# Tokens gathered as rows in f32, y scattered in two f32r halves, glu columns finished first: one change to the expert stage of a hybrid attention and mixture-of-experts block

## The chip, the cores and the metric

The kernel runs on one core of a Trainium2 chip. The metric is the time of one execution on the device in microseconds (us). The kernel before takes 1219.95 us, the median of 3 runs (1217.81 to 1220.06).

The engines: PE (TensorE) multiplies, PEld is its weight load, DVE is VectorE, ACT is ScalarE, POOL is GpSimd. SP issues nearly all of the big transfers (DMA).

## The reference

One layer: RMSNorm, a projection into forgetting attention, short convolution and cross-attention, their gated merge into x1, then a mixture of experts. The change touches the mixture and what chooses its tokens.

```python
def clamped_swiglu(h):
    glu, lin = h[..., :D_FF], h[..., D_FF:]
    glu = jnp.minimum(glu, SWIGLU_LIMIT)
    lin = jnp.clip(lin, -SWIGLU_LIMIT, SWIGLU_LIMIT)
    return glu * jax.nn.sigmoid(SWIGLU_ALPHA * glu) * (lin + 1.0)

def moe(x2, w_router, b_router, w_up, b_up, w_down, b_down):
    logits = (x2 @ w_router + b_router).astype(jnp.float32)
    top_vals, top_idx = lax.top_k(logits, TOP_K)
    top_w = jax.nn.softmax(top_vals, axis=-1)
    combine = ...                       # top_w at the chosen experts, 0 elsewhere
    out = jnp.zeros_like(x2)
    for e in range(N_EXPERTS):
        a = clamped_swiglu(x2 @ w_up[e] + b_up[e])
        out = out + combine[:, e:e + 1] * (a @ w_down[e] + b_down[e])
    return out

h2 = rms_norm(x1, norm2_g, NORM_EPS).reshape(B * S, D)     # return x1 + moe(h2, ...)
```

Sizes: 256 tokens, D = 1024, 32 experts with d_ff = 1024, 4 experts to a token, all in f32. The weights of one expert are 12 MiB.

## The kernel before

**Stages.** The first 270 us or so are the dense part: pieces of weights are loaded, split into f32r halves (`w_hi`, `w_lo`) and multiplied as hi x hi + lo x hi + hi x lo. Then come the routing and the experts.

**The ring.** Expert weights stream through a ring of 11 slots of 2 MiB in SBUF. A chunk fills a slot. An expert is 6 chunks: 4 of `w_up` (two of the eight row blocks k = 0..7 each, 2048 columns: 1024 glu, 1024 lin) and 2 of `w_down` (four row blocks each). SP issues the 192 loads in order. Load g waits until PE has finished with load g - 11, and a load is otherwise bound by nothing. Slots 0 to 9 are taken from buffers of the dense part as these fall free. The eleventh holds `h2T` and `x1s`, and its first load waits for the routing to be done with them (`parts_pool`, `parts_dve`).

**The routing** (lines 1110 to 1190 on DVE). DVE waits for the logits, takes the top 8 (`max`), their indices (`max_index`), casts these to f32 (L1129), builds one-hot rows for four experts and sums them to `chosen`. PE turns `chosen` into positions with a triangular product. `pos_tab` then holds each token's place in each expert's list of 64 slots. `more` is the number of further lists that experts with over 64 tokens need. The trace has 32 lists, so there were none.

**One item** is one expert's list of 64 slots. PE's order of work in `item` (L1590):

1. Up product, k = 0..7: for each k the glu and the lin columns, two halves of 512 each. The 64 slots of a half take 64 output partitions, so two matmuls stand side by side (`bank_glu`, `bank_lin`).
2. Behind k = 6, `gather` (L1537) for the next item: tokens of x1, scaled and split in three bf16 parts (`m_parts`), times the one-hot `pick`. It is 48 matmuls of 64 columns, and gives the features on partitions at once (`bank_cy`), which DVE moves to `xgT` with the norm's gain (L1164).
3. `scatter` (L1587) of the item before into three of its four output banks: the token weights `pick_wT` (f32) times `y_sb` (f32).
4. Transposes of the activated rows `sig` to `aT` (L1635), which wait for `a_ready`. Then the fourth bank's scatter, two transposes of `pick_w` (L1644), the bias rows (L1650), and the down product (L1661) of 16 matmuls.

**Activation between 3 and 4.** When all of the up product is done (`up_done`), DVE clamps glu (L1224), clamps lin (L1225), multiplies (lin + 1) with glu (L1228), and multiplies with ACT's Sigmoid (L1232), which signals `a_ready`. ACT's round is: Sigmoid, copy of `aT`, copy of `pick_wT`, copy of `y_sb`. DVE and ACT run items in a hardware loop, PE's 32 items are written out. Each engine runs its instructions in the order written, and waits on semaphores.

## Time and profile before

| | |
|---|---|
| median of 3 runs | 1219.95 us |
| the profiled execution's own time | 1219.87 us |
| its span (first to last instruction) | 1218.1 us |
| PE busy | 1169.7 us (96%) |
| DVE, ACT, POOL busy | 339.1, 266.9, 84.7 us |
| PE's granted clock, mean over the span | 0.978 |
| DMA | 450.16 MB; 427 to 428 GB/s from 330 us to 1150 us |
| chain that ended last | PE 85%, DVE 10%, ACT 2% |

A busy PE is not PE at its peak: matmuls overlap, and their ends are modelled. Read an item by the starts of its groups, which add up without gaps. A matmul in f32 shows as two records. "Granted clock" is 1.0 at 2.4 GHz and 0.5 at 1.2 GHz. An item starts with its first L1604 matmul: 288.76 us for the first, 1211 us is the end of the last down product.

### The profile page before, as it was taken

The numbers are of one execution on the slowest core, as the hardware profiler recorded it, in microseconds if no ns is written. First come the engines' busy times: TensorE is split into PE (matmuls) and PEld (weight loads), VectorE is DVE, ScalarE is ACT, GpSimd is POOL, SyncE is SP. The second block draws the span as 40 slices with busy tenths as digits, with TensorE's granted clock in tenths as the row PEclk, the third lists the DMA queues.
The fourth block names the chain that finished last, engine by engine and source line by source line (L and its number), as shares of the span: only waits on it lengthen the run. The fifth ranks groups of instructions, "written<-read, shape, count | busy, mean of one in ns | idle before, by whom it ended". The sixth has DMA issues, their size and how long they took to land.

```text
span 1218.1 us, 15891 instructions
## 1 busy us (share of the span) xinstructions
PE 1169.7 (96%) x6786; PEld 562.5 (46%) x6788; DVE 339.1 (28%) x625; ACT 266.9 (22%) x407; POOL 84.7 (7%) x101
## 2 busy tenths in 40 slices
PE   8999999997999999999999999999999999999998
PEld 7789988884333333333333333333333333333332
DVE  5767865655111111111111111111121111111112
ACT  6765454442111111111111111111111111111110
POOL 6333340001000000000000000000000000000000
PEclk9999999998999999999999999999999999999999
DMA  8454469858999999999999999999999999999991
GB/s 313 151 169 149 151 246 361 304 217 330 382 425 429 428 428 428 427 428 426 429 427 427 428 428 429 426 427 428 427 428 428 427 427 428 428 426 427 428 405 66
DMA packets 51476, 450.16 MB, mean 370 GB/s; under 512 B 4610, under 2 KB 4738, under 8 KB 26836
## 3 DMA queue, kind: packets, MB, share of 16 engines
q1 hardware_dynamic: 49936, 447.76, 89.1%
q10 hardware_dynamic: 1476, 1.42, 0.4%
q8 instruction: 55, 0.90, 0.3%
q14 instruction: 9, 0.07, 0.0%
HBM read 448.12 MB, written 1.05 MB: 369 GB/s over the span
## 4 chain that ended last, share of the span: by engine, by line
PE 85%; DVE 10%; ACT 2%; issue 1%; POOL 1%; DMA 0%; DVEq 0%; SPq 0%; POOLq 0%; ACTq 0%
PE aux L1604 37%; PE aux L1661 20%; PE acc L1448 11%; PE aux L1537 4%; PE acc L1441 3%; PE acc L1587 3%; PE aux L1635 2%; DVE lin L1228 2%; DVE sig L1232 2%; DVE glu L1224 2%; DVE lin L1225 2%; PE aux L1615 1%; DVE w_lo L880 1%; PE aux L1650 1%; PE aux L1644 1%
## 5 line engine op out<-in xcount | busy, mean ns | idle before, releaser
L1604 PE MATMUL aux<-ring,xgT 128*64 128x512 f32 x2048 | 458.2, 594 | 0.8 <-DVE xgT L1164 0.8
L1604 PEld LDWEIGHTS aux<-ring,xgT 128*64 128x64 f32 x2048 | 140.5, 137 | 266.4 <-issue 258.0
L1661 PE MATMUL aux<-ring,aT 128*64 128x512 f32 x1024 | 245.3, 635 | 0.0
L1224 DVE TENSOR_SCALAR glu<-aux 128x512 f32<-128x512 f32 x32 | 22.1, 692 | 483.3 <-PE aux L1604 483.3
L1661 PEld LDWEIGHTS aux<-ring,aT 128*64 128x64 f32 x1024 | 77.0, 147 | 148.7 <-issue 147.1
L845 ACT ACTIVATE sig<-glu 128x512 f32<-128x512 f32 x32 | 20.1, 630 | 474.9 <-DVE glu L1224 474.9
L880 DVE TENSOR_TENSOR w_lo<-raw,w_hi 128x1024 fp32r<-128x1024 f32 x80 | 104.3, 1324 | 50.0 <-ACT w_hi L662 50.0
L662 ACT ACTIVATE w_hi<-raw 128x1024 fp32r<-128x1024 f32 x80 | 84.1, 1059 | 88.6 <-PE acc L1448 73.0
L1587 PE MATMUL acc<-y_sb,pick_wT 64*128 64x512 f32 x256 | 98.2, 628 | 0.8 <-ACT y_sb L853 0.8
L1448 PE MATMUL acc<-w_hi,hT_hi 128*128 128x512 f32 x188 | 75.7, 403 | 1.4 <-DVE hT_lo L892 1.3
L1448 PE MATMUL acc<-w_hi,hT_lo 128*128 128x512 f32 x188 | 73.3, 390 | 0.0
L1448 PE MATMUL acc<-w_lo,hT_hi 128*128 128x512 f32 x188 | 73.2, 390 | 0.0
L1160 DVE TENSOR_SCALAR bias_sel<-ones_bf,exp_sel 96x64 bf16<-96x64 bf16 x33 | 7.8, 237 | 233.0 <-PE aux L1661 233.0
L853 ACT ACTIVATE y_sb<-aux 128x512 f32<-128x512 f32 x32 | 19.1, 598 | 238.1 <-PE aux L1661 238.1
L1537 PEld LDWEIGHTS aux<-pick,m_parts 128*128 128x128 bf16 x1584 | 49.2, 99 | 26.9 <-issue 26.0
L1537 PE MATMUL aux<-pick,m_parts 128*128 128x64 bf16 x1584 | 53.1, 195 | 0.4 <-DVE pick L1150 0.4
L1635 PE MATMUL aux<-ident,sig 128*128 128x128 f32 x128 | 24.0, 310 | 30.2 <-DVE sig L1232 30.2
L1587 PEld LDWEIGHTS acc<-y_sb,pick_wT 64*128 64x128 f32 x256 | 30.8, 185 | 45.8 <-issue 42.1
L1635 PEld LDWEIGHTS aux<-ident,sig 128*128 128x128 f32 x128 | 17.9, 209 | 56.0 <-DVE sig L1232 56.0
L845 ACT ACT_TABLE_LOAD x32 | 41.1, 1283 | 0.6
L1448 PEld LDWEIGHTS acc<-w_hi,hT_hi 128*128 128x128 f32 x188 | 35.3, 188 | 9.4 <-issue 1.6
L1448 PEld LDWEIGHTS acc<-w_hi,hT_lo 128*128 128x128 f32 x188 | 35.3, 188 | 7.6
(292 smaller groups left out, 920.1 us busy)
## 6 DMA issues: line engine op xcount, KB each, us to landing
ring<-w_up_dram SPq DMA_DIRECT2D x128, 2048.0 KB, 22.9
ring<-w_down_dram SPq DMA_DIRECT2D x64, 2048.0 KB, 21.9
raw<-w_in_dram SPq DMA_DIRECT2D x25, 1024.0 KB, 5.2
raw<-w_branch_dram SPq DMA_DIRECT2D x6, 1024.0 KB, 5.2
raw<-w_kv_dram SPq DMA_DIRECT2D x4, 1024.0 KB, 5.2
raw<-w_out_dram SPq DMA_DIRECT2D x4, 1024.0 KB, 5.3
x<-x_dram SPq DMA_DIRECT2D x2, 512.0 KB, 4.3
raw<-w_in_dram SPq DMA_DIRECT2D x2, 512.0 KB, 6.4
```

The costliest lines, as they stand in the source:

```text
L662: nc.scalar.activation(w_hi[:, s % 4], raw[:, p % 4, 2 * h:2 * h + 2], ACT.Copy).then_inc(hi_done, 1)
L845: nc.scalar.activation(sig[:], glu[:], ACT.Sigmoid, scale=ALPHA).then_inc(sig_ready, 1)
L880: nc.vector.tensor_tensor(w_lo[:, s % 4], raw[:, p % 4, 2 * h:2 * h + 2], plain_f32(w_hi[:, s % 4]), ALU.subtract).then_inc(lo_done, 1)
L1224: nc.vector.tensor_scalar(glu[:], bank_glu[:], LIMIT, None, ALU.min).then_inc(glu_ready, 1)
L1225: nc.vector.tensor_scalar(lin[:], bank_lin[:], LIMIT, -LIMIT, ALU.min, ALU.max).then_inc(up_read, 1)
L1441: ins = nc.tensor.matmul(dst, w_[:, cs], a_[:, k], start=opening and m == 0 and c % 2 == 0, stop=closing and m == 2, skip_group_check=True)
L1448: ins = nc.tensor.matmul(banks[t][:], a_[:, k, ts], w_, start=opening and m == 0 and kind != "gate", stop=closing and m == 2)
L1537: ins = nc.tensor.matmul(bank_cy[:, k * SLOTS:(k + 1) * SLOTS], up_rows(m_parts[:, m, t], k), pick[:, t], start=(t == 0 and m == 0 and k = ...
L1587: nc.tensor.matmul(acc[b][:], pick_wT[s, t], y_sb[s, :], start=False, stop=True, skip_group_check=True).then_inc(scattered, 1)
L1604: ins = nc.tensor.matmul(bank[64 * half:64 * half + 64, :], xgT[:, k], w_rows[:, c0 + half * W:c0 + (half + 1) * W], start=(k == 0), stop= ...
L1635: ins = nc.tensor.transpose(bank_t[:, j * P:(j + 1) * P], sig[:].rearrange("s (p j) -> s j p", j=DOWN_ROWS)[:, j], ident[:])
L1661: ins = nc.tensor.matmul(bank_cy[64 * half:64 * half + 64, :], aT[:, j, 64 * ff_half:64 * ff_half + 64], w_rows[:, half * W:(half + 1) * W ...
```

## The change

- **Gather by tokens.** `pick` is now f32 and carries the token's `rstd`. It is the stationary operand, x1 itself in f32 is the moving one: 4 matmuls of 512 columns that give the 64 rows of the list (`bank_cy`). ACT copies them to SBUF (`xg_tok`, the same memory as `sig`), PE turns them with 4 transposes, and DVE moves them to `xgT`. The parts `m_parts`, `x1s` and what built them are gone. The gather for the next item stands behind k = 3, the turn behind k = 5.
- **Glu first.** For the last chunk (k = 6, 7) all glu columns come first and signal `glu_done`, then the lin columns, which signal `up_done`. DVE clamps glu, multiplies it with the Sigmoid, and only then clamps lin, in PSUM, and multiplies.
- **Scatter in f32r halves.** ACT writes y scaled with the slot's weight as `y_hi`, DVE the remainder as `y_lo`. The stationary operand is the 0/1 matrix `pickT` in f32r. It is 8 f32r matmuls, all ahead of the transposes of `sig`. They belong to the item before, which was so before too.
- **The transposes of `pick_w`** move into the middle of the down product; DVE makes `pickT` and `slot_w` from them.
- **Chosen by match-replace.** The four chosen logits are overwritten with a marker, and a comparison gives `chosen`. Softmax is taken over all 32 logits and masked.
- **A twelfth slot**, in the memory that `hT_lo`, `merged` and `m_parts` had. `hT_lo` and `merged` move into slot 10, which is first loaded behind the last dense product. Slot 11 waits for `logits_ready`.

ACT's loop, one round, before: the row that loads a function table stands at the head and has no wait in front of it.

```order
L855 UNCONDITIONAL_BRANCH
L845 ACT_TABLE_LOAD
L845 ACTIVATE sig<-glu 128x512 [waits glu_ready]
L847 ACTIVATE aT<-aux 128x512 [waits aT_done]
L849 REGISTER_ALU [waits pick_wT_done]
L850 ACTIVATE pick_wT<-aux 128x256 [waits scattered]
L853 ACTIVATE y_sb<-aux 128x512 [waits y_done]
L855 REGISTER_ALU
L855 COMPARE_AND_BRANCH
```

The same loop after the change:

```order
L827 ISA
L812 ACT_TABLE_LOAD
L812 ACTIVATE sig<-aux 128x512 [waits gathered]
L820 ACT_TABLE_LOAD [waits glu_ready]
L820 ACTIVATE sig<-glu 128x512 [waits xg_turned]
L822 ACTIVATE aT<-aux 128x512 [waits aT_done]
L825 ACTIVATE y_hi<-aux,slot_w 128x512 [waits y_done,pickT_ready]
L827 REGISTER_ALU
L827 COMPARE_AND_BRANCH
```

There are now two table rows in a round, one for the copy at the head and one for the Sigmoid. The second is behind the wait for `glu_ready`, and the Sigmoid itself waits for `xg_turned`.

PE, the second item of before from the gather to the bias rows of the down product:

```order
L1537 MATMUL aux<-pick,m_parts 128x64 [waits y_ready,pick_ready]
L1537 MATMUL aux<-pick,m_parts 128x64 x47
L1604 MATMUL aux<-ring,xgT 64x512 x4
L1587 MATMUL acc<-y_sb,pick_wT 128x512 [waits pick_wT_ready,y_ready]
L1587 MATMUL acc<-y_sb,pick_wT 128x512 x2
L1635 MATMUL aux<-ident,sig 128x128 [waits pick_wT_ready,a_ready]
L1635 MATMUL aux<-ident,sig 128x128 x3
L1587 MATMUL acc<-y_sb,pick_wT 128x512 [waits pick_wT_ready,y_ready]
L1644 MATMUL aux<-ident,pick_w 128x128 [waits aT_ready,pick_w_ready]
L1644 MATMUL aux<-ident,pick_w 128x128
L1650 MATMUL aux<-bias_down,bias_sel 64x512 [waits xg_ready]
L1650 MATMUL aux<-bias_down,bias_sel 64x512
```

PE, the second item after the change, from the end of the up product into the down product (`acc` are the four output banks):

```order
L1551 MATMUL acc<-y_hi,pickT 128x512 [waits y_lo_ready,y_hi_ready,pickT_ready]
L1551 MATMUL acc<-y_hi,pickT 128x512
L1551 MATMUL acc<-y_lo,pickT 128x512 x2
L1551 MATMUL acc<-y_hi,pickT 128x512 x2
L1551 MATMUL acc<-y_lo,pickT 128x512 x2
L1613 MATMUL aux<-ident,sig 128x128 [waits a_ready]
L1613 MATMUL aux<-ident,sig 128x128 x3
L1619 MATMUL aux<-bias_down,bias_sel 64x512 [waits xg_ready]
L1619 MATMUL aux<-bias_down,bias_sel 64x512
L1631 MATMUL aux<-ring,aT 64x512 [waits slot_loaded10,aT_ready]
L1631 MATMUL aux<-ring,aT 64x512 x7
L1642 MATMUL aux<-ident,pick_w 128x128 [waits pick_w_ready]
```

The scatter is whole and ahead of `a_ready`. Nothing but the two bias rows stands between the transposes of `sig` and the down product, which now waits for `aT_ready` itself. The first row of the `pick_w` transposes is behind eight matmuls of the down product.

PE, the same item's up product after the change, from k = 2:

```order
L1561 MATMUL aux<-ring,xgT 64x512 [waits slot_loaded7]
L1561 MATMUL aux<-ring,xgT 64x512 x7
L1494 MATMUL aux<-x_50,pick 64x512 [waits pick_ready,y_lo_ready,y_hi_ready]
L1494 MATMUL aux<-x_50,pick 64x512 x3
L1561 MATMUL aux<-ring,xgT 64x512 [waits slot_loaded8]
L1561 MATMUL aux<-ring,xgT 64x512 x7
L1506 MATMUL aux<-ident,sig 128x128 [waits xg_tok_ready]
L1506 MATMUL aux<-ident,sig 128x128 x3
L1561 MATMUL aux<-ring,xgT 64x512 [waits slot_loaded9]
L1561 MATMUL aux<-ring,xgT 64x512 x7
```

The gather (L1494) and the turn (L1506) stand between groups of matmuls of the up product. The last group of eight is glu, then lin, of k = 6 and 7.

The diff, cut to its core (names of semaphores, memory and routing tables are left out where the list above says it):

```diff
             sp.wait_ge(half_used, 2 * NP)
-            load_next(8)
-            load_next(9)
+            for g in (8, 9, 10):
+                load_next(g)
             sp.wait_ge(logits_ready, 1)
-            sp.wait_ge(parts_pool, 2)
-            sp.wait_ge(parts_dve, 2)
-            load_next(10)
+            load_next(11)
...
+            def copy_gathered(n):
+                act.wait_ge(gathered, n)
+                nc.scalar.activation(xg_tok[:], bank_cy[:], ACT.Copy).then_inc(xg_tok_ready, 1)
+
+            copy_gathered(1)
 
             def item(n):
+                copy_gathered(n + 1)
+                act.wait_ge(xg_turned, n + 1)
                 act.wait_ge(glu_ready, n)
                 nc.scalar.activation(sig[:], glu[:], ACT.Sigmoid, scale=ALPHA).then_inc(sig_ready, 1)
                 act.wait_ge(aT_done, n)
                 nc.scalar.activation(aT[:].rearrange("p k s -> p (k s)"), bank_t[:], ACT.Copy).then_inc(aT_ready, 1)
-                act.wait_ge(pick_wT_done, n)
-                act.wait_ge(scattered, 4 * n)
-                nc.scalar.activation(pick_wT[:].rearrange("p t s -> p (t s)"), bank_t[:, 0:NT * P],
-                                     ACT.Copy).then_inc(pick_wT_ready, 1)
+                act.wait_ge(pickT_ready, n)
                 act.wait_ge(y_done, n)
-                nc.scalar.activation(y_sb[:], bank_cy[:], ACT.Copy).then_inc(y_ready, 1)
+                nc.scalar.activation(y_hi[:], bank_cy[:], ACT.Copy, scale=slot_w[:, 0:1]).then_inc(y_hi_ready, 1)
 
...
+            nc.vector.tensor_scalar(ntop[:], top_v[:, :, 0], -1.0, None, ALU.mult).then_inc(top_ready, 1)
+
+            chained(nc.vector.memset(top_v[:, :, TOPK:8], HUGE))
             for t in range(NT):
-                ins = nc.vector.max_index(top_i[:, t], top_v[:, t], logits[:, t])
+                ins = nc.vector.match_replace(out=others[:, t], in_to_replace=top_v[:, t], in_values=logits[:, t],
+                                              imm_value=-HUGE)
             chained(ins)
-            chained(nc.vector.tensor_copy(top_f[:], top_i[:]))
+            nc.vector.tensor_scalar(chosen3[:, :, 0], others[:], -HUGE, None, ALU.is_equal).then_inc(chosen_ready, 1)
+            dve.wait_ge(chosen_ready, 1)
+            chosen = chosen3[:, :, 0]
...
             def item(n):
 
+                dve.wait_ge(glu_done, n)
+                nc.vector.tensor_scalar(glu[:], bank_glu[:], LIMIT, None, ALU.min).then_inc(glu_ready, 1)
+                dve.wait_ge(glu_ready, n)
+                dve.wait_ge(sig_ready, n)
+                nc.vector.tensor_tensor(sig[:], glu[:], sig[:], ALU.mult).then_inc(gated_ready, 1)
                 dve.wait_ge(up_done, n)
-                nc.vector.tensor_scalar(glu[:], bank_glu[:], LIMIT, None, ALU.min).then_inc(glu_ready, 1)
-                nc.vector.tensor_scalar(lin[:], bank_lin[:], LIMIT, -LIMIT, ALU.min, ALU.max).then_inc(up_read, 1)
-                dve.wait_ge(glu_ready, n)
-                dve.wait_ge(up_read, n + 1)
-                nc.vector.scalar_tensor_tensor(lin[:], lin[:], 1.0, glu[:], ALU.add, ALU.mult
-                                               ).then_inc(glin_ready, 1)
-                dve.wait_ge(glin_ready, n)
-                dve.wait_ge(sig_ready, n)
-                nc.vector.tensor_tensor(sig[:], lin[:], sig[:], ALU.mult).then_inc(a_ready, 1)
-
-                dve.wait_ge(gathered, n + 1)
-                move_gathered()
+                nc.vector.tensor_scalar(bank_lin[:], bank_lin[:], LIMIT, -LIMIT, ALU.min, ALU.max
+                                        ).then_inc(lin_ready, 1)
+                dve.wait_ge(gated_ready, n)
+                dve.wait_ge(lin_ready, n)
+                nc.vector.scalar_tensor_tensor(sig[:], bank_lin[:], 1.0, sig[:], ALU.add, ALU.mult
+                                               ).then_inc(a_ready, 1)
+
+                move_gathered(n + 1)
+                build_pick_w(bass.ds(n - 1, 1))
                 build_pick(bass.ds(n + 1, 1))
+
                 dve.wait_ge(pick_wT_done, n)
-                build_pick_w(bass.ds(n, 1))
+                nc.vector.tensor_scalar(pickT[:].rearrange("p t s -> p (t s)"), bank_t[:, 0:NT * P], 0.0, None,
+                                        ALU.is_gt)
+                nc.vector.tensor_reduce(slot_w[:], bank_t[:, 0:NT * P], AX, ALU.add).then_inc(pickT_ready, 1)
                 dve.wait_ge(y_done, n)
                 build_bias_sel(bass.ds(n, 1))
+                dve.wait_ge(pickT_ready, n)
+                dve.wait_ge(y_hi_ready, n)
+                nc.vector.scalar_tensor_tensor(y_lo[:], bank_cy[:], slot_w[:, 0:1], plain_f32(y_hi[:]),
+                                               ALU.mult, ALU.subtract).then_inc(y_lo_ready, 1)
 
             with dve.Fori(1, NEXP + 1) as n:
...
-            def gather(first_item=False):
-
+
+            def gather(n):
+
+                pe.wait_ge(pick_ready, n)
                 for t in range(NT):
-                    for m in range(3):
-                        if first_item and t == 1 and m == 2:
-                            pe.wait_ge(parts_dve, 2)
-                        for k in range(KD):
-                            ins = nc.tensor.matmul(bank_cy[:, k * SLOTS:(k + 1) * SLOTS],
-                                                   up_rows(m_parts[:, m, t], k), pick[:, t],
-                                                   start=(t == 0 and m == 0 and k == 0),
-                                                   stop=(t == NT - 1 and m == 2), skip_group_check=True)
+            def turn_gathered(n):
+
+                pe.wait_ge(xg_tok_ready, n)
+                for q in range(KD // 2):
+                    c, j = q // UP_ROWS, q % UP_ROWS
+                    n = UP_ROWS * P
+                    rows = xg_tok[:, c * n:(c + 1) * n].rearrange("s (p j) -> s j p", j=UP_ROWS)[:, j]
+                    ins = nc.tensor.transpose(bank_cy[:, q * P:(q + 1) * P], rows, ident[:])
+                ins.then_inc(xg_turned, 1)
...
-            def scatter(items, banks):
-
-                pe.wait_ge(y_ready, items)
-                pe.wait_ge(pick_wT_ready, items - 1)
-                for b in banks:
-                    t, half = b // 2, b % 2
-                    s = slice(64 * half, 64 * half + 64)
-                    nc.tensor.matmul(acc[b][:], pick_wT[s, t], y_sb[s, :],
...
+            def scatter(n, opening=False):
+
+                pe.wait_ge(pickT_ready, n)
+                pe.wait_ge(y_hi_ready, n)
+                pe.wait_ge(y_lo_ready, n)
+                for t in range(NT):
+                    for part in (y_hi, y_lo):
+                        for half in range(2):
+                            s = slice(64 * half, 64 * half + 64)
+                            ins = nc.tensor.matmul(acc[2 * t + half][:], pickT[s, t], part[s, :],
+                                                   start=opening and part is y_hi, stop=True, skip_group_check=True)
+                            if part is y_lo:
+                                ins.then_inc(scattered, 1)
...
+                    if k == 3:
+                        if not first_item:
+                            pe.wait_ge(y_hi_ready, n - 1)
+                            pe.wait_ge(y_lo_ready, n - 1)
+                        gather(n + 1)
+                    if k == 5:
+                        turn_gathered(n + 1)
+
+                c = UP_CHUNKS - 1
+                pe.wait_ge(slot_loaded[slot_of[c]], loads[c])
+                for bank, c0, done in ((bank_glu, 0, glu_done), (bank_lin, FF, up_done)):
+                    for k in range(KD - UP_ROWS, KD):
+                        ins = up_product(k, bank, c0)
+                    ins.then_inc(done, 1)
 
                 if not first_item:
-                    scatter(n, range(3))
...
+                pe.wait_ge(aT_ready, n)
```

## Rows read from the trace of the kernel before

**Rows 1.** Stretches, all engines: items 3, 4, 2 to 32, two early gaps.

```profile
core 0: us, PE busy (x) PEld busy (x) DVE busy (x) ACT busy (x) POOL busy (x), PEclk, DMA share, GB/s
347.70:377.45 29.75, 28.82 (x168) 10.44 (x165) 4.44 (x10) 3.49 (x5) 0.00 (x0) 0.94 1.01 428
377.45:405.50 28.05, 27.12 (x168) 10.01 (x165) 4.44 (x10) 3.49 (x5) 0.00 (x0) 1.00 1.01 428
319.71:1211.00 891.29, 862.38 (x5086) 317.26 (x5082) 137.58 (x310) 108.27 (x155) 0.00 (x0) 0.98 0.98 417
282.00:290.00 8.00, 4.88 (x58) 3.57 (x61) 6.01 (x21) 2.97 (x8) 0.50 (x1) 0.57 0.54 187
...
314.00:320.00 6.00, 6.00 (x30) 1.96 (x28) 0.00 (x0) 0.07 (x1) 0.00 (x0) 1.00 0.59 183
```

**Rows 2.** PE in order of time, item 4: start, us, line, what, count, idle.

```profile
390.00 1.57 PE L1537 MATMUL aux<-pick,m_parts 128*128 128x64 bf16 x48
391.50 1.94 PE L1604 MATMUL aux<-ring,xgT 128*64 128x512 f32 x8
393.37 1.98 PE L1587 MATMUL acc<-y_sb,pick_wT 64*128 64x512 f32 x6
396.29 0.75 PE L1635 MATMUL aux<-ident,sig 128*128 128x128 f32 x4 [0.93 <-DVE sig L1232]
...
398.63 7.03 PE L1661 MATMUL aux<-ring,aT 128*64 128x512 f32 x32
405.50 1.02 PE L1604 MATMUL aux<-ring,xgT 128*64 128x512 f32 x4
```

**Rows 3.** ACT in order of time, the same item.

```profile
377.66 0.60 ACT L853 ACTIVATE y_sb<-aux 128x512 f32<-128x512 f32 x1 [8.23 <-PE aux L1661]
378.28 1.28 ACT L845 ACT_TABLE_LOAD   x1
394.21 0.63 ACT L845 ACTIVATE sig<-glu 128x512 f32<-128x512 f32 x1 [14.65 <-DVE glu L1224]
397.07 0.60 ACT L847 ACTIVATE aT<-aux 128x512 f32<-128x512 f32 x1 [2.23 <-PE aux L1635]
```

**Rows 4.** DVE in order of time, the same item.

```profile
393.49 0.69 DVE L1224 TENSOR_SCALAR glu<-aux 128x512 f32<-128x512 f32 x1 [15.48 <-PE aux L1604]
394.10 0.68 DVE L1225 TENSOR_SCALAR lin<-aux 128x512 f32<-128x512 f32 x1
394.81 0.69 DVE L1228 SCALAR_TENSOR_TENSOR lin<-lin,glu 128x512 f32<-128x512 f32 x1
395.54 0.69 DVE L1232 TENSOR_TENSOR sig<-lin,sig 128x512 f32<-128x512 f32 x1
```

**Rows 5.** PE in order of time, f32r matmuls of the dense part.

```profile
263.17 0.39 PE L1448 MATMUL acc<-w_lo,hT_hi 128*128 128x512 f32 x1
263.39 0.39 PE L1448 MATMUL acc<-w_hi,hT_lo 128*128 128x512 f32 x1
```

**Rows 6.** DVE in order of time, in the routing.

```profile
280.15 0.40 DVE L1120 SCALAR_TENSOR_TENSOR logits<-acc,rstd,spread 128x32 f32<-128x32 f32 x2
...
281.36 1.17 DVE L1129 CAST top_f<-top_i 128x16 f32<-128x16 uint32 x1
```

**Rows 7.** PE in order of time, from the router to the first expert.

```profile
275.11 1.94 PE L1486 MATMUL acc<-wr,h2T 128*128 128x32 f32 x16 [0.25 <-DVE h2T L1102]
...
285.24 2.74 PE L1537 MATMUL aux<-pick,m_parts 128*128 128x64 bf16 x48 [0.44 <-DVE pick L1150]
288.76 1.12 PE L1604 MATMUL aux<-ring,xgT 128*64 128x512 f32 x2 [0.78 <-DVE xgT L1164]
```

**Rows 8.** ACT in order of time, the last copy of y.

```profile
1211.04 0.60 ACT L853 ACTIVATE y_sb<-aux 128x512 f32<-128x512 f32 x1 [6.75 <-PE aux L1661]
```

**Rows 9.** The last load into the ring: its issue, and its time to landing.

```profile
L452 SPq DMA_DIRECT2D ring<-w_down_dram x1: 327/327/327, 1157.1 to 1157.1; - x1
...
DMA to landing us min/median/max: 36.0/36.0/36.0
```

More of the change, by code:

```diff
@@ L1552, in list_first @@
+            turn_gathered(1)
             def list_first():
@@ L1590, in item @@
-            def item(n, slot_of, loads, between={}):
-                first_item = bool(between)
+            def scatter(n, opening=False):
[4 more added lines that the diff above has]
+                    for part in (y_hi, y_lo):
+                        for half in range(2):
+                            s = slice(64 * half, 64 * half + 64)
[3 more added lines that the diff above has]
+                                ins.then_inc(scattered, 1)
@@ new lines, in item, with up_product @@
+            def item(n, slot_of, loads, first_item=False, second_item=False):
+                def up_product(k, bank, c0):
+                    w_rows = ring[:, slot_of[k // UP_ROWS]].rearrange("p (j n) -> p j n", j=UP_ROWS)[:, k % UP_ROWS]
+                    for half in range(2):
+                        ins = nc.tensor.matmul(bank[64 * half:64 * half + 64, :], xgT[:, k],
+                                               w_rows[:, c0 + half * W:c0 + (half + 1) * W],
+                                               start=(k == 0), stop=(k == KD - 1), skip_group_check=True)
+                    return ins
```

264 lines of the change are left out of this document (101 added, 163 removed).

## The prediction

> **What bounds the kernel now.** I read four views in this order: the slices of the page, the stretches, the order of time of one item, and the ring's loads.
>
> The stretches first [rows 1]. Items 2 to 32 take 891.29 us of the 1218.1 us span, with PE busy for 862.38 us and the DMA engines at a share of 0.98. So both limits are near. Item 4, at a granted clock of 1.00, takes 28.05 us. Item 3 has a mean clock of 0.94 and takes 29.75 us. 31 items at 28.05 would be 869.6 us, so the clock costs 21.7 us, or some 13 drops of 1.70 us each.
>
> The item [rows 2]. PE never waits for a chunk. Its one wait with a releaser is at 396.29, where the transposes of `sig` wait 0.93 us for DVE. The last up product ends at 391.50 + 1.94 = 393.44, and the transposes start 2.85 us later. In those 2.85 us lies the chain of four DVE operations [rows 4], with ACT's Sigmoid beside it [rows 3]. The three banks of scatter cover some 2 us of it. So PE sets the pace, and inside an item it is the chain from the end of the up product to `a_ready`.
>
> The other limit is close. The last load is issued at 1157.1 and lands 36.0 us later, at 1193.1 [rows 9], while PE's last down product ends at 1211 [rows 8]. An item's 12 MiB (12.58 MB) at the 428 GB/s of [rows 1] take 29.4 us, more than the item on PE, which the queue of issued loads makes up for so far. So a faster PE would gain only until it meets the transfers.
>
> **The change part by part.** All sums are against the profiled execution: 1219.87 us, 1.8 us more than its span, and within 0.1 us of the median 1219.95. A matmul of the product kind (f32, 512 columns, two side by side) costs (405.50 - 398.63) / 16 = 0.43 us [rows 2].
>
> *Before, one item at full clock, by starts* [rows 2]: gather 391.50 - 390.00 = 1.50; from the last product's slot to the transposes 396.29 - 393.37 = 2.92; from there to the down product 398.63 - 396.29 = 2.34; all else 28.05 - 6.76 = 21.29.
>
> *Gather and turn.* Four matmuls of the product kind, 4 x 0.43 = 1.72 us. Four transposes, 0.75 us as the ones at 396.29, and 0.05 for the edges: 0.80. ACT's copy between them takes 0.60 us [rows 3] and has two k (3.4 us) of products as cover, so it is free. The wait of the gather for `y_lo` is free too: y is ready some 1.5 us into the item, the gather comes after 7 us. Bounds for the turn: 0.75 to 1.0.
>
> *From the glu columns to `a_ready`.* This is the step that decides. The listing of ACT's loop shows a table row behind the wait for `glu_ready`. In the trace of before the table load takes 1.28 us, but it starts at 378.28, right behind the copy of y and 15 us ahead of the Sigmoid [rows 3]. Now it stands in the chain. From `glu_done`: clamp of glu 0.69, table load 1.28, Sigmoid 0.63, product with glu 0.69, clamp of lin 0.68, last product 0.69, and six handoffs of 0.03 to 0.05 as in [rows 3, 4], less the 0.07 that back-to-back DVE rows overlap (393.49 to 394.10): 4.84 us. DVE waits in order, so the clamp of lin, whose input has long been there, also stands behind the load. Glu is done four matmuls, 1.72 us, before the end of the up product. From that end to the transposes it is 4.84 - 1.72 = 3.12 us, against 2.85 before. So that step is 2.92 + 0.27 = 3.19. The head start of 1.72 and the shorter tail are eaten by the load. The clamp in PSUM is not in the trace; 0.4 (a small one) to 0.9 bounds it, I take the 0.68 of the PSUM to SBUF one.
>
> *Scatter.* Eight f32r matmuls at a spacing of 263.39 - 263.17 = 0.22 us [rows 5] are 1.8 us, or 0.9 if the two halves, which use different rows of the array, run side by side. Both fit in the 3.12 us. Cost nothing; and the fourth bank (about 1.06 of the 2.34) is gone from behind the transposes. But it was that matmul that covered ACT's copy of `aT`.
>
> *Transposes to down product.* ACT starts 397.07 - 396.29 = 0.78 after the transposes, copies 0.60, handoff 0.05: 1.43 us, with the bias rows inside. Before 2.34.
>
> *Transposes of `pick_w` inside the down product.* Half of the four at 396.29, 0.37, and two edges: 0.50 (0.37 to 0.7).
>
> *New item at full clock:* 21.29 + 1.72 + 0.80 + 3.19 + 1.43 + 0.50 = 28.93 us, so **+0.88 us** an item and +28.2 us for 32. With the bounds of the terms it is +0.4 to +1.3.
>
> *Clock.* Before, an item has one gap of 0.93 us without a matmul, and 13 of 31 items show a drop. Now the gaps are 3.12 - 1.8 = 1.3 us ahead of the transposes and about 0.5 us (0.78 + 0.60 + 0.05 less 0.67 of transposes and 0.25 of bias rows) behind them: 1.8 us within 4.6 us. In proportion that is 1.9 x 13/31 = 0.8 of the items, 25 drops, 12 more at 1.67 us: **+20.0 us**. Bounds: none more (0) and one in every item (19 more, +31.7).
>
> *Start.* The router's products end at 275.11 + 1.94 = 277.05 [rows 7], but DVE takes the logits at 280.15 [rows 6], since it is busy with the parts: -3.1. The cast goes, -1.2 [rows 6]. One-hot, sum and index over 256 columns give way to operations on 64, about -0.9. The gather falls from 2.74 (at the half clock) to 1.72, -1.0 [rows 7]. Copy, turn and handoffs are new, +1.5. Sum **-4.7 us** (-2 to -6). The first up product then starts near 284 instead of 288.76.
>
> *End.* Behind the last copy of y comes one DVE operation and its handoff, +0.75, and 1.8 us of scatter instead of 2.0: **+0.6 us**.
>
> *The twelfth slot* lets loads start earlier: shares of 0.54 in 282 to 290 and 0.59 in 314 to 320 [rows 1] are 3.7 + 2.5 = 6.2 us of idle transfers. It is worth nothing while PE sets the pace, and 6.2 us if the transfers do. DVE's and POOL's other operations (`pickT`, `slot_w`, `pick_w`) have 3 us and more of the down product as cover.
>
> *Sum:* 1219.87 - 4.7 + 28.2 + 20.0 + 0.6 = **1264 us**.
>
> *A rule beside it.* In the trace the copy of y ends at 378.26 and the load starts at 378.28 and is over after 1.28 [rows 3], so there is no drain to be seen. The Trainium skill (ScalarE: Activation LUTs, What ACT_TABLE_LOAD costs) gives the same 1283 ns and adds about 1380 ns of drain for each switch. By that the chain would be 1.38 us longer and the sum would be 1308 us. The trace does not bear it out.
>
> **The rivals.**
>
> *The load isn't in the chain* (it costs nothing when run, or goes ahead of the wait). Then the chain is 3.56 us, the scatter just fills the 1.84 us behind the up product, and an item is 27.65 us at full clock. PE then meets the transfers: the last load lands at 1193.1 - 6.2 = 1186.9, then half a down product (3.4 us) and what follows 1211 now (7.1 + 0.6 us) give 1198.0 of span, **1200 us**. For it speaks that a reload for a copy seems needless, against it the listing, in which a load at the head of the loop and one behind `glu_ready` are real rows, and that each such row of before shows as 1.28 us. The Trainium skill (ScalarE: Activation LUTs, Table sets: the hidden batching unit) says that cheap functions such as the copy are in every set; by that one set would do, and this rival's time would hold. No row here shows a copy that runs in the Sigmoid's set and loads nothing.
>
> *The clock takes no more than before.* The item is longer but the drops stay 13: 1264 - 20 = **1244 us**. For it: two short gaps may count for less than one long one, and the later start of the down product moves the gaps about. Against it: the time without a matmul doubles.
>
> *The clock falls in every item, or twice in some.* If the halves of the scatter run side by side, the first gap is 2.2 us. One in each item gives **1276 us**, a few twice up to 1285.
>
> *Terms that cancel.* The item grows only by 0.2 (turn and transposes overlap, a fast clamp) and the drops stay: 1219.9 - 4.7 + 6.4 + 0.6 = 1222 us.
>
> **How the numbers follow.** The forecast of 1264 (1252 to 1272) has 0.50. Clock as before: 0.20. Clock in every item or more, drain included: 0.17. Terms that cancel: 0.04. The load out of the chain: 0.09. A difference below 0.2%, 2.4 us, can't be told from none here. Faster holds the load's rival: 0.09. No difference: 0.03, out of the terms that cancel. The rest, 0.88, is slower. The range of 1228 to 1280 leaves out the rival at 1200, the no-change case and the highest times, together some 0.16. Its low end is the sum with the low bound of the item (+0.4, 12.8 us) and no added drop.
>
> **What would show each step.** The profile after should have a table load between the clamp of glu and the Sigmoid in each item, PE's idle time ahead of the transposes of `sig` with releaser DVE at 1.1 to 1.4 us (or 2 us, if the scatter's halves overlap), and some 0.5 us ahead of the down product with releaser ACT. Item starts at full clock should be 28.9 us apart and the mean clock over the items 0.95 to 0.96. At some 30.3 us an item, over the transfers' 29.4, the DMA share should fall below 1, and a load should land in 8 to 15 us late in the run too: the ring then waits for PE. The first up product should start near 284. If instead PE waits for chunks late in the run and loads take 40 us and more to land, the transfers bound it and the forecast is wrong. It is wrong too if the table load runs ahead of `glu_ready`, or if the clock stays at 1.0.

## The result and the profile after

| | median us | range | runs |
|---|---|---|---|
| before | 1218.88 | 1217.57 to 1220.06 | 4 |
| after | 1282.73 | 1281.22 to 1283.16 | 4 |

The ratio is 1.0522, with a 95% interval of 1.0504 to 1.0540: 63.8 us slower. The forecast was 1264 us, the range 1228 to 1280. The direction was right. The time lies 2.7 us above the range.

The page of the kernel after (engines' busy time with count, then the slices; in the groups, busy us and mean ns of one, then idle time and its releaser; for the loads, KB and median us to landing). Its own time is 1281.22 us:

```profile
span 1279.4 us, 13646 instructions
...
PE 1182.9 (92%) x5596; PEld 549.9 (43%) x5596; DVE 380.8 (30%) x711; ACT 313.6 (25%) x432; POOL 80.2 (6%) x98
...
DMA  8545489679999999999999999999999999999900
...
L820 ACT ACT_TABLE_LOAD x32 | 41.1, 1283 | 198.5 <-DVE glu L1180 198.5
...
ring<-w_up_dram SPq DMA_DIRECT2D x128, 2048.0 KB, 12.3
```

PE is busy for 92% of the span instead of 96%. The table load stands in each of the 32 items behind `glu`, and costs 1283 ns. A load of the ring lands 12.3 us after its issue: the ring waits for PE now, and PE for no transfer.

The stretches of the kernel after (item 2, and items 2 to 32; columns as in [rows 1]), to be held against the 28.05, 29.75 and 891.29 us of [rows 1]:

```profile
318.88:349.60 30.72, 28.22 (x130) 9.95 (x128) 5.98 (x13) 5.08 (x6) 0.00 (x0) 0.94 0.98 409
318.88:1271.40 952.52, 874.91 (x3970) 307.14 (x3966) 185.55 (x403) 157.45 (x186) 0.00 (x0) 0.94 0.93 387
```

All 31 items are 30.72 to 30.74 us long (952.52 / 31 = 30.73), and all have a mean clock of 0.94. Before, only some had.

PE in order of time over an item of the kernel after, from its turn of the gathered rows to the next item (start, us, line, what, count, idle), the counterpart of [rows 2]:

```profile
449.11 1.89 PE L1494 MATMUL aux<-x,pick 128*64 128x512 f32 x8
450.83 3.60 PE L1561 MATMUL aux<-ring,xgT 128*64 128x512 f32 x16
454.36 0.74 PE L1506 MATMUL aux<-ident,sig 128*128 128x128 f32 x4
455.04 3.65 PE L1561 MATMUL aux<-ring,xgT 128*64 128x512 f32 x16
458.62 0.50 PE L1551 MATMUL acc<-y_hi,pickT 64*128 64x512 f32 x2
458.95 0.40 PE L1551 MATMUL acc<-y_lo,pickT 64*128 64x512 f32 x2
459.19 0.40 PE L1551 MATMUL acc<-y_hi,pickT 64*128 64x512 f32 x2
459.42 0.40 PE L1551 MATMUL acc<-y_lo,pickT 64*128 64x512 f32 x2
461.98 0.75 PE L1613 MATMUL aux<-ident,sig 128*128 128x128 f32 x4 [2.16 <-DVE sig L1189]
462.65 0.41 PE L1619 MATMUL aux<-bias_down,bias_sel 96*64 96x512 bf16 x2
463.41 5.35 PE L1631 MATMUL aux<-ring,aT 128*64 128x512 f32 x16 [0.35 <-ACT aT L822]
468.69 0.44 PE L1642 MATMUL aux<-ident,pick_w 128*128 128x128 f32 x2
469.06 3.65 PE L1631 MATMUL aux<-ring,aT 128*64 128x512 f32 x16
```

Two things are to be seen. The eight matmuls of the scatter start in pairs, 0.24 us apart, so they are over after 1.2 us, and PE then waits 2.16 us. And the first eight down matmuls (16 records) take 5.35 us, the second eight 3.65: the slow stretch of the clock lies in the first half of the down product. Its granted clock, ahead of it, in it and behind it (columns as in [rows 1]):

```profile
462.00:463.70 1.70, 1.35 (x8) 0.84 (x10) 1.47 (x5) 0.60 (x1) 0.00 (x0) 0.98 0.97 414
464.00:467.00 3.00, 3.00 (x10) 0.96 (x8) 0.00 (x0) 0.00 (x0) 0.00 (x0) 0.50 1.02 431
467.10:470.00 2.90, 2.90 (x16) 0.86 (x14) 0.76 (x2) 0.00 (x0) 0.00 (x0) 1.00 1.00 356
```

PE works at 1.2 GHz instead of 2.4 right after the two waits, and that costs 5.35 - 3.65 = 1.70 us. Such a stretch at the lower clock is called a drop here. Without it an item takes 30.72 - 1.70 = 29.02 us.

ACT and DVE over the same stretch, the counterpart of [rows 3, 4]:

```profile
457.79 1.28 ACT L820 ACT_TABLE_LOAD   x1 [6.15 <-DVE glu L1180]
459.08 0.63 ACT L820 ACTIVATE sig<-glu 128x512 f32<-128x512 f32 x1
462.76 0.60 ACT L822 ACTIVATE aT<-aux 128x512 f32<-128x512 f32 x1 [3.04 <-PE aux L1613]
```

```profile
457.02 0.69 DVE L1180 TENSOR_SCALAR glu<-aux 128x512 f32<-128x512 f32 x1 [13.38 <-PE aux L1561]
459.82 0.69 DVE L1183 TENSOR_TENSOR sig<-glu,sig 128x512 f32<-128x512 f32 x1 [2.11 <-ACT sig L820]
460.43 0.69 DVE L1185 TENSOR_SCALAR aux<-aux 128x512 f32<-128x512 f32 x1
461.23 0.69 DVE L1189 SCALAR_TENSOR_TENSOR sig<-aux,sig 128x512 f32<-128x512 f32 x1
```

This is the chain as forecast: clamp of glu, load, Sigmoid, three DVE operations, 461.98 - 457.02 = 4.96 us to the transposes.

Start and end (PE, the first gather, the first up product, the last scatter), the counterparts of [rows 7, 8]:

```profile
279.71 3.42 PE L1494 MATMUL aux<-x,pick 128*64 128x512 f32 x8 [0.72 <-DVE pick L1111]
...
285.36 1.94 PE L1561 MATMUL aux<-ring,xgT 128*64 128x512 f32 x8 [0.79 <-DVE xgT L1129]
...
1273.43 0.50 PE L1551 MATMUL acc<-y_hi,pickT 64*128 64x512 f32 x2 [1.80 <-DVE y_lo L1204]
```

The spans differ by 1279.4 - 1218.1 = 61.3 us. Start: 285.36 - 288.76 = -3.4. Item 1: (318.88 - 285.36) - (319.71 - 288.76) = +2.6. Items 2 to 32: 952.5 - 891.3 = +61.2. End: (1279.4 - 1271.4) - (1218.1 - 1211.0) = +0.9. Within the +61.2, 31 items are 29.02 - 28.05 = 0.97 us longer at full clock, 30.1 us. The drops are 31 x 1.70 = 52.7 us against 21.7 before, +31.0. Item 1 has a drop in both kernels.

### The profile page after: what moved, and what is told of

Read it like the earlier page. It is cut to its first block, busy times and chain, and to the rows that moved or that the text cites. A ratio compares the mean times of both kernels' runs of the same rounds, so it can differ in the third digit from the quotient of the medians.

```text
span 1279.4 us, 13646 instructions
## 1 busy us (share of the span) xinstructions
PE 1182.9 (92%) x5596; PEld 549.9 (43%) x5596; DVE 380.8 (30%) x711; ACT 313.6 (25%) x432; POOL 80.2 (6%) x98
## 4 chain that ended last, share of the span: by engine, by line
PE 80%; DVE 10%; ACT 8%; issue 2%; POOL 1%; DMA 0%; DVEq 0%; ACTq 0%; SPq 0%; POOLq 0%
PE aux L1561 31%; PE aux L1631 22%; PE acc L1413 11%; PE aux L1494 5%; ACT L820 3%; PE acc L1406 3%; PE aux L1613 2%; DVE sig L1189 2%; DVE glu L1180 2%; DVE sig L1183 2%; PE aux L1506 2%; ACT sig L820 2%; DVE aux L1185 2%; ACT aT L822 2%; PE aux L1581 1%
## 5 line engine op out<-in xcount | busy, mean ns | idle before, releaser
L1561 PE MATMUL aux<-ring,xgT 128*64 128x512 f32 x2048 | 463.5, 594 | 0.8 <-DVE xgT L1129 0.8
L1631 PE MATMUL aux<-ring,aT 128*64 128x512 f32 x1024 | 288.0, 714 | 11.2 <-ACT aT L822 11.2
L1561 PEld LDWEIGHTS aux<-ring,xgT 128*64 128x64 f32 x2048 | 143.7, 137 | 264.3 <-issue 253.8
L1631 PEld LDWEIGHTS aux<-ring,aT 128*64 128x64 f32 x1024 | 80.0, 160 | 177.7 <-issue 157.0
L825 ACT ACTIVATE y_hi<-aux,slot_w 128x512 fp32r<-128x512 f32 x32 | 22.0, 687 | 302.7 <-PE aux L1631 302.7
L820 ACT ACT_TABLE_LOAD x32 | 41.1, 1283 | 198.5 <-DVE glu L1180 198.5
L812 ACT ACTIVATE sig<-aux 128x512 f32<-128x512 f32 x33 | 19.7, 597 | 231.5 <-PE aux L1494 231.5
L1197 DVE TENSOR_SCALAR pickT<-aux 128x256 fp32r<-128x256 f32 x32 | 13.6, 424 | 182.0 <-PE aux L1642 182.0
L1494 PE MATMUL aux<-x,pick 128*64 128x512 f32 x264 | 63.8, 605 | 0.7 <-DVE pick L1111 0.7
L822 ACT ACTIVATE aT<-aux 128x512 f32<-128x512 f32 x32 | 19.1, 597 | 97.4 <-PE aux L1613 97.4
L1183 DVE TENSOR_TENSOR sig<-glu,sig 128x512 f32<-128x512 f32 x32 | 22.2, 693 | 67.4 <-ACT sig L820 67.4
L812 ACT ACT_TABLE_LOAD x32 | 41.1, 1283 | 0.6
## 6 DMA issues: line engine op xcount, KB each, us to landing
ring<-w_up_dram SPq DMA_DIRECT2D x128, 2048.0 KB, 12.3
```

What stands on the lines that cost most here:

```text
L812: nc.scalar.activation(xg_tok[:], bank_cy[:], ACT.Copy).then_inc(xg_tok_ready, 1)
L820: nc.scalar.activation(sig[:], glu[:], ACT.Sigmoid, scale=ALPHA).then_inc(sig_ready, 1)
L822: nc.scalar.activation(aT[:].rearrange("p k s -> p (k s)"), bank_t[:], ACT.Copy).then_inc(aT_ready, 1)
L1183: nc.vector.tensor_tensor(sig[:], glu[:], sig[:], ALU.mult).then_inc(gated_ready, 1)
L1494: ins = nc.tensor.matmul(bank_cy[64 * half:64 * half + 64, :], pick[:, t], x1[:, t, half * W:(half + 1) * W], start=(t == 0), stop=(t == N ...
L1561: ins = nc.tensor.matmul(bank[64 * half:64 * half + 64, :], xgT[:, k], w_rows[:, c0 + half * W:c0 + (half + 1) * W], start=(k == 0), stop= ...
```

## The experiments

All stand against runs of the kernel before on the same chip (median 1217.86 to 1218.05). The theory: the longer item comes from the table load in the chain, and the rest from the clock, which falls in proportion to PE's idle time. The rivals: the load costs nothing there, or the clock falls in each item whatever the size of the gap.

**The load ahead of the wait.** ACT's two waits are exchanged. In the kernel after, the load stood behind the one that is written second, `glu_ready`; with the order turned round it stands behind `xg_turned`, which comes earlier.

```diff
-                act.wait_ge(xg_turned, n + 1)
                 act.wait_ge(glu_ready, n)
+                act.wait_ge(xg_turned, n + 1)
```

> The changed kernel with ACT's two waits ahead of the Sigmoid swapped, so that the table load stands behind xg_turned and no longer behind glu_ready. Theory (the load of 1.28 us is in the chain, and the longer gap makes the clock fall in every item): the chain from glu_done to the transposes falls from 4.96 to 3.7 us, the gap on PE from 2.3 to about 1.0 us, an item at full clock is 27.7 us, the drops fall to 13 of 31 or fewer, and the transfers bound the stage: 1200 us (1193 to 1212), DMA share 1.0, last loads landing after 40 us and more. Rival (the load isn't what makes the item long; gather, turn and the uncovered copy of aT are): only a few us less, 1265 to 1280 us.

Measured: 1200.78 us (1198.17 to 1201.96), ratio 0.9849 (0.9828 to 0.9869). Two waits exchanged turn +5.2% into -1.5%. ACT in this kernel, then PE:

```profile
470.72 1.28 ACT L820 ACT_TABLE_LOAD   x1 [3.54 <-PE aux L1506]
473.28 0.63 ACT L820 ACTIVATE sig<-glu 128x512 f32<-128x512 f32 x1 [1.28 <-DVE glu L1180]
```

```profile
476.17 0.75 PE L1613 MATMUL aux<-ident,sig 128*128 128x128 f32 x4 [0.81 <-DVE sig L1189]
...
477.61 3.65 PE L1631 MATMUL aux<-ring,aT 128*64 128x512 f32 x16 [0.35 <-ACT aT L822]
```

The load is over before `glu_ready` comes. The gap falls from 2.16 to 0.81 us, and the down product runs at full clock. The stretches (one item, and the items up to 1060 us):

```profile
457.35:485.05 27.70, 26.54 (x131) 9.51 (x129) 5.99 (x13) 5.08 (x6) 0.00 (x0) 1.00 1.01 428
315.00:1060.00 745.00, 710.31 (x3418) 254.35 (x3418) 157.39 (x342) 135.85 (x160) 0.00 (x0) 1.00 1.01 427
```

An item is 27.70 us, 1.32 less than the 29.02, which is the load of 1.28. None of items 2 to 32 has a drop. 32 x 1.32 + 31 x 1.70 = 95 us would come back, and 82 did, since the transfers now bound the end: from item 25 on an item takes 29.4 us, what its 12 MiB take at 428 GB/s. PE's waits for loads over the whole span (us, times, longest):

```profile
PE aux L1561 <- DMA ring<-w_up_dram: 9.4, 17, 1.1
```

**The gap filled.** The kernel after, with matmuls of no use between the scatter and the wait for `a_ready`:

```diff
+                    for _ in range(9):
+                        nc.tensor.matmul(bank_t[:], ones_bf[0:96], bias_up[:, 0:W], start=True, stop=True)
```

> The changed kernel with nine bf16 matmuls of 512 columns (ones times the bias rows, into the bank that the transposes of sig then overwrite) between the scatter and the wait for a_ready, items 2 to 32. They add no result. The chain stays as it is, the gap of 2.3 us is filled with 9 x 0.22 = 1.95 us of matmuls. Theory (the gap makes the clock fall, 1.71 us an item): items 29.0 us apart without drops, 1281 - 31 x 1.71 = 1228 us. Rival (the drop has another cause, say the wait for aT or the period of the item): 30.7 us apart as before, 1282 us; if the matmuls delay the transposes, more.

Measured: 1229.78 us (1228.94 to 1231.54), ratio 1.0097 (1.0079 to 1.0115).

```profile
453.51 2.12 PE L1610 MATMUL aux<-bias_up,ones_bf 96*128 96x512 bf16 x9
455.73 0.75 PE L1615 MATMUL aux<-ident,sig 128*128 128x128 f32 x4
```

The work of an item, its chain and its length at full clock are as in the kernel after. Only the time without a matmul is gone (0.10 us of it is left ahead of the transposes), and 1282.7 - 1229.8 = 52.9 us with it, against 31 x 1.70 = 52.7. Items 2 to 32 have no drop and are 29.04 us long. So the clock costs 53 us here. What is left over the kernel before (1229.78 - 1217.94 = 11.8 us) is the longer item, the start and the end, less the 21.7 us that the kernel before loses by its own drops.

**The scatter in another order**, all of one row half first (DVE's last adds then wait for the whole scatter, which is left out here):

```diff
-                for t in range(NT):
-                    for part in (y_hi, y_lo):
-                        for half in range(2):
+                for half in range(2):
+                    for t in range(NT):
+                        for part in (y_hi, y_lo):
```

> The changed kernel with the eight scatter matmuls in another order: the four of one half, then the four of the other, so that two that use the same rows of the array follow each other. (The last adds wait for all of the scatter.) Chain unchanged. Theory of the forecast (matmuls of different rows ran side by side, 0.24 us a pair, which made the gap 2.3 instead of 1.3 us, and the number of drops goes with the length of the gap): scatter 1.8 us, gap 1.3 to 1.4 us, 20 to 26 drops instead of 31, items 29.0 us at full clock, 1263 to 1275 us. Rival (any gap over a certain length costs a drop in each item): 1282 us. Rival (below that length none or few): 1235 to 1250 us.

Measured: 1282.81 us (1281.54 to 1284.01), ratio 1.0526 (1.0507 to 1.0544). It did not do what it was meant to:

```profile
461.62 0.41 PE L1551 MATMUL acc<-y_lo,pickT 64*128 64x512 f32 x2
464.18 0.75 PE L1613 MATMUL aux<-ident,sig 128*128 128x128 f32 x4 [2.15 <-DVE sig L1189]
```

The scatter still took 1.2 us and the gap stayed at 2.15, so the run tests nothing about the length of the gap. It does say that PE puts the matmuls of the two row halves side by side in this order too. The Trainium skill (TensorEngine Tiling (Array Packing), Key Properties) says that tiles of the array operate independently of each other, and both traces agree, with 0.24 us from pair to pair. The trace of the kernel before already showed it. Its first two banks of scatter, one of each row half, take 1.13 us together, and the third bank alone adds 0.85 to make the 1.98 of [rows 2]:

```profile
393.37 1.13 PE L1587 MATMUL acc<-y_sb,pick_wT 64*128 64x512 f32 x4
```

**The load put into the chain of the kernel before:**

```diff
+                act.wait_ge(up_done, n)
                 act.wait_ge(glu_ready, n)
```

> The kernel before with a second wait (up_done) ahead of the Sigmoid, which puts its table load behind glu_ready; nothing else. Theory (the load alone makes a chain long): the product with the Sigmoid starts 2.75 us after the end of the up product instead of 2.1, so the transposes start 0.66 us later, the gap grows from 0.93 to 1.6 us, items 28.7 us at full clock (+21 us), and the clock falls in 22 to 31 of 31 items instead of 13 (+15 to +31 us): 1255 to 1271 us. Rival (DVE hides the load, or it costs nothing here): 1219 us. Rival (chain longer but no more drops): 1240 us.

Measured: 1265.53 us (1264.30 to 1268.65), ratio 1.0396 (1.0374 to 1.0417). Three stretches of one item each, without a drop, with one of twice the length and with one:

```profile
400.32:429.12 28.80, 27.12 (x165) 10.11 (x165) 4.44 (x11) 3.49 (x5) 0.00 (x0) 1.00 1.00 420
368.25:400.32 32.07, 30.39 (x164) 10.71 (x164) 4.43 (x11) 3.49 (x5) 0.00 (x0) 0.89 0.97 404
409.53:439.92 30.39, 28.71 (x168) 10.48 (x166) 4.44 (x10) 3.49 (x5) 0.00 (x0) 0.94 1.00 423
```

```profile
400.32 0.75 PE L1636 MATMUL aux<-ident,sig 128*128 128x128 f32 x4 [1.68 <-DVE sig L1233]
```

The gap goes from 0.93 us to 1.68, the item from 28.05 to 28.80: 32 x 0.75 = 24 us. The clock takes about as much again: of items 2 to 32, 10 have no drop, 16 have one and 5 have one of twice the length, as in the second row (3.3 us). That is 21 items with a drop, against 13 before. The gap is 1.68 us in all of them, with a drop and without. The load at this place is thus enough for 3.9%, with no other part of the change.

**Part of the gap filled**, with four matmuls, then six (the same edit, with 4 and 6 for the 9):

> The changed kernel with four instead of nine of the filling bf16 matmuls between scatter and a_ready (0.9 us; they add no result), which leaves the gap of 1.3 us that the prediction had reckoned with. Theory of the forecast (a drop count in proportion to the gap: the step failed only because the scatter took 1.0 and not 1.8 us): 20 to 28 drops, 1258 to 1276 us. Rival (the rule of proportion itself was wrong, upwards): a drop in each item still, 1282 us. Rival (wrong downwards; the kernel with the early load had a gap of 0.8 us and no drops): 1230 to 1250 us.

> As the kernels with nine and four filling matmuls, with six: the gap ahead of the transposes is 0.75 us, the one behind them 0.35 us as before, the chain and the item (29.0 us at full clock) are the same. So far: gaps of 1.18 and 0.35 us with a drop in all 31 items, gaps of 0.1 and 0.35 with none, and the early load with 0.81 and 0.35 with none. Theory (there is a length of idle time below which no item has a drop, and above which, at this item length, each has): none, 1230 us. Rival (in proportion after all, with a steeper rule): some 10 to 20 drops, 1247 to 1264 us.

Measured with four: 1282.84 us (1282.26 to 1283.42), ratio 1.0532 (1.0513 to 1.0551). With six, in two runs: 1230.81 us (1230.54 to 1231.09), ratio 1.0106 (1.0076 to 1.0135). The transposes of `sig`, with four:

```profile
463.63 0.75 PE L1615 MATMUL aux<-ident,sig 128*128 128x128 f32 x4 [1.18 <-DVE sig L1189]
```

and with six:

```profile
456.98 0.75 PE L1615 MATMUL aux<-ident,sig 128*128 128x128 f32 x4 [0.75 <-DVE sig L1189]
```

Halving the gap gives back nothing: a drop in each of items 2 to 32, as with 2.16 us. Another 0.43 us off, and all of these drops go. In this kernel the clock's cost is a step in the gap, not a slope. It is no rule for the gap alone: the kernel before with the load in its chain has a gap of 1.68 us, well above this step, and 10 of its 31 items have no drop.

**The second gap closed as well:** the four, and one more behind the bias rows.

```diff
+                    for _ in range(4):
+                        nc.tensor.matmul(bank_t[:], ones_bf[0:96], bias_up[:, 0:W], start=True, stop=True)
...
+                nc.tensor.matmul(bank_glu[:], ones_bf[0:96], bias_up[:, 0:W], start=True, stop=True)
```

> Four filling matmuls ahead of the transposes (gap 1.18 us, with which each item had a drop) and one behind the bias rows, in the wait for aT (0.35 us falls to some 0.13 us), written to the bank of glu, which the next item starts anew. Theory (idle time of both gaps together counts: 1.31 us, between the 1.16 us without drops and the 1.53 us with one in each item): fewer drops, 1230 to 1262 us. Rival (the gap ahead of the transposes alone counts): 1282 us.

Measured, in two runs: 1283.07 us (1282.94 to 1283.20), ratio 1.0535 (1.0504 to 1.0565).

```profile
465.21 5.35 PE L1634 MATMUL aux<-ring,aT 128*64 128x512 f32 x16
```

The wait ahead of the down product is gone, and the drop is still there (5.35 us). With 1.18 us ahead of the transposes, closing the other gap changes nothing. That doesn't settle which of them counts: PE is still idle for 1.21 us of an item here, and was for 27.70 - 26.54 = 1.16 in the kernel with the early load, which has no drops in items 2 to 32. So whether the first gap or the sum of both counts stays open.

**The glu columns given no head start.** The kernel with the early load, and DVE's clamp of glu waits for all of the up product, as in the kernel before:

```diff
-                dve.wait_ge(glu_done, n)
+                dve.wait_ge(up_done, n)
```

> The kernel with the early table load, with DVE's clamp of glu waiting for up_done instead of glu_done; PE's order stays. It takes away what glu first gives. Theory (the chain from the end of the up product sets the gap): transposes 1.72 us later, gap 2.5 us, items 29.4 us at full clock and a drop in each, 31.1 us apart: 1200 -> 1285 to 1300 us. Rival (the chain is covered by something else): 1200 to 1215 us.

Measured: 1282.53 us (1281.81 to 1283.45), ratio 1.0528 (1.0509 to 1.0547). The head start is worth 81.7 us where the load is out of the chain, drops included. The expected 1285 to 1300 was missed, though the chain is longer than in the kernel after:

```profile
464.83 0.75 PE L1613 MATMUL aux<-ident,sig 128*128 128x128 f32 x4 [2.53 <-DVE sig L1189]
465.51 0.62 PE L1619 MATMUL aux<-bias_down,bias_sel 96*64 96x512 bf16 x2
466.27 4.98 PE L1631 MATMUL aux<-ring,aT 128*64 128x512 f32 x16
```

The slow stretch begins earlier here and lies partly in waiting time (the bias rows take 0.62 us instead of 0.41), so the down product loses 4.98 - 3.65 = 1.33 us instead of 1.70. By as much as the gap is longer (2.53 - 2.16 = 0.37 us) the drop is cheaper, and the item is 30.72 us again. It came to that by steps: item 2 takes 31.03 us, item 3 30.87, item 4 30.80, and from item 9 on all take 30.72. Items 2 and 10:

```profile
320.83:351.86 31.03, 28.15 (x130) 9.89 (x128) 5.98 (x13) 5.08 (x6) 0.00 (x0) 0.95 0.98 406
567.21:597.93 30.72, 28.07 (x130) 9.85 (x128) 5.99 (x13) 5.08 (x6) 0.00 (x0) 0.94 0.99 411
```

**The ring with 11 slots**, in the kernel with the early load (the memory of the twelfth stays unused):

```diff
-RING = 12
+RING = 11
...
-            sp.wait_ge(logits_ready, 1)
-            load_next(11)
```

> The kernel with the early table load, with the ring back at 11 slots (the memory of the twelfth stays unused). Theory (12 slots let the early transfers run without a break, 6 us, and the transfers set the end of this version): last landing 3 to 7 us later than with 12 slots, 1204 to 1208 us. Rival (PE sets the pace for most of the run and the transfers only late, so the idle transfers are made up for): 1200 to 1202 us.

Measured: 1202.97 us (1202.71 to 1205.14), ratio 0.9882 (0.9864 to 0.9901). It is 2.2 us over the kernel with twelve, whose own runs reach from 1198.2 to 1202.0. The last load lands at 1138.8 + 49.5 = 1188.3 instead of 1136.5 + 51.0 = 1187.5. Both ranges expected were missed, the rival's (1200 to 1202) by 1 us. The twelfth slot is worth some 2 us at most even where transfers bind, on two chips and hardly clear of the scatter of the runs, and not the 6.2 of the prediction.

**The kernel before with its gap filled**, four matmuls behind the three banks of scatter:

```diff
+                    for _ in range(4):
+                        nc.tensor.matmul(bank_t[:], ones_bf[0:96], bias_up[:, 0:W], start=True, stop=True)
```

> The kernel before with four filling bf16 matmuls (0.87 us, into the bank that the transposes overwrite; they add no result) behind the three banks of scatter, where PE waits 0.93 us for DVE. Theory (its 13 drops come from that gap and cost 21.7 us): items 28.05 us apart, clock near 1.0, and the transfers then set the end: last landing 1193 us, then half a down product and 7 us: 1200 to 1208 us. Rival (the drops have another cause): 1218 us, 13 drops as before.

Measured: 1208.93 us (1208.83 to 1210.64), ratio 0.9925 (0.9907 to 0.9943), 0.9 us over the upper end expected. The 13 drops are gone, worth 21.7 us, but only 9.1 arrive: here too the items grow to 29.4 us, from item 27 on, with the transfers as the bound. PE's waits for loads in this kernel:

```profile
PE aux L1604 <- DMA ring<-w_up_dram: 10.5, 10, 1.2
```

The last load is issued at 1145.6 and lands 48.4 us later, at 1194.0, 6.5 us after that of the kernel with the early load. That accounts for most of the 8.2 us between the two. Which part of the change lets its transfers finish earlier (the slots that no longer wait for the routing's buffers, or the earlier start) was argued, not measured.

## Why the prediction was right in its direction and short by 19 us

- **The item at full clock: right.** Forecast 28.93 us, measured 29.02. Of its terms, gather 450.83 - 449.11 = 1.72 (1.72); the turn 455.04 - 454.36 = 0.68 (0.80); from the end of the up product's slot to the transposes 461.98 - 458.62 = 3.36 (3.19); from there to the down product 1.43 (1.43); the transposes of `pick_w` 469.06 - 468.69 = 0.37 (0.50). The clamp in PSUM takes 0.69 (0.68 taken). Single terms are off by up to 0.17 us in both directions, and the rest of the item is 0.17 us longer than the 21.29 taken, so that the sum comes out within 0.09 is in part luck. That the table load stands in the chain, and costs its 1.28 us, is shown from both sides: taking it out gives 1.32 us an item back, putting it into the kernel before adds 0.75 there, where the load overlaps part of the DVE operations.
- **The step that failed is the clock's:** "In proportion that is 1.9 x 13/31 = 0.8 of the items, 25 drops, 12 more at 1.67 us: +20.0 us." It was 18 more, +31.0 us. The cost of a drop was right (1.70 against 1.67), the count was not. Two things were wrong in it. The gap was mis-sized: the scatter ran in pairs, which made the two gaps 2.16 + 0.35 = 2.51 us instead of 1.8, and by the prediction's own proportion that would have been 2.7 x 13/31, a drop in each item. And the rule of proportion itself was wrong for this kernel: with four filling matmuls the gaps are 1.18 + 0.35 = 1.53 us, for which it gives some 21 drops, and there were 31. Of the kernels made from the one after, those with gaps of 0.10, 0.75 and 0.81 us ahead of the transposes had no drop in items 2 to 32, those with 1.18 to 2.53 had one in each. The rival that put one drop into each item had the right count, and named the scatter in pairs as its reason, at a chance of only 0.17.
- **That rival's own 1276 us** was 6.7 us short. The start gave 3.4 us instead of 4.7, mostly because the first gather still ran at half clock (3.42 us, 1.72 taken; granted clock 0.55 from 279.71 to 283.06). Item 1 cost 2.6 us instead of 0.9. 31 items were 0.09 us longer, 2.8 us. The end was 0.3 us longer. The profiled run is 1.5 us under the median. These are some 7.6 us; the rival had taken 19 drops more and not 18, which gives 0.7 back.
- **The load's rival** was wrong for this kernel and right as a price: 1200 us worked out, 1200.78 measured for the kernel that really has the load out of the chain.
- **The twelfth slot** is worth nothing while PE sets the pace, as forecast: no wait of PE for a load is in the trace of the kernel after. The run that took it away was of the kernel with the early load, not of this one.

What remains open: what decides between 0.81 us (no drop) and 1.18 us (always) in this kernel, and why the kernel before drops in 13 of 31 items with 0.93 us and in only 21 of 31 with 1.68. Its items were 28.05 and 28.80 us long at full clock, those of the kernel after 29.04. The length of the item, or where the gap falls in time, thus seems to count beside the length of the gap. No run changed either with the gap held fixed, so it is not shown.

The kernel with the two waits exchanged beats both, at 1200.78 us against 1217.94 for the kernel before on the same chip.

## What to carry to other kernels

- Where a function table is reloaded in each round of a loop, the wait behind which the load lands is part of the design: look at its row in the listing. In the kernel after, the kernel with the early load and the kernel before with the late one, two waits are written ahead of the Sigmoid, and each time the load stood behind the second. So write last, directly ahead of the activation, the wait whose event comes early, and the late one before it. Here the order of two waits was worth 82 us.
- Don't spread the price of PE's clock in proportion over its idle time. In this kernel a gap cost nothing (up to 0.81 us) or a drop in each round (from 1.18 us on); in the kernel before, gaps of 0.93 and 1.68 us cost a drop in some rounds only. So a small growth of a gap can cost more than the gap itself, a reduction that ends above the step gives nothing, and matmuls of no use in the gap are a cheap test (here -53 us).

## What the runs showed of the hardware that was not expected

- **Items of unlike chains came to one period.** Five kernels with gaps of 2.53, 2.16, 2.15 and 1.18 us (twice) have medians of 1282.5 to 1283.1 us, all with items 30.72 to 30.74 us apart (the first few of the one with 2.53 us excepted), though one of them needs 30.72 - 1.33 = 29.39 us at full clock and the others 29.02. What holds them there was not tested. The Trainium skill (TensorE: Matmul & The Clock Gate, A second HAM failure mode: psum-queue depth-cycling) tells of a kernel whose short idle times between groups of matmuls make the clock go up and down; the traces here agree, with 1.18 us in a 29 us item as the shortest gap that did it each time. They also show that the gap alone doesn't decide it: with 1.68 us in an item of 28.80 us the clock fell in 21 of 31.
- **Half-array matmuls pair up in both orders of issue that were tried**, 0.24 us a pair, also where four of one half are issued ahead of four of the other.
- **With many loads outstanding, the issue itself takes long.** In the kernel with the early load, SP's last issues take 4.24 us instead of 0.33, and the loads land 50 us later; the rate is 428 GB/s from 1090 to 1140 us. In the kernel before, where loads from 1095 us on landed after 32 to 38 us, and in the kernel after (9.5 to 13.4 us), each issue took 0.33. That a full queue holds SP up is an inference from this:

```profile
L445 SPq DMA_DIRECT2D ring<-w_down_dram x2: 4238/4239/4240, 1132.2 to 1136.5; - x2
...
DMA to landing us min/median/max: 50.4/50.7/51.0
```

- **A table load shows no drain in the kernel after either**, as the prediction had read it before: 457.79 + 1.28 = 459.07, and the Sigmoid starts at 459.08.
